# Attention weights of a hybrid decoder turned by transposing DMAs, mask by a maximum in the scan, q, k, v evicted by ScalarE

## The reference, cut to what matters

```python
p = h @ w_in                       # q, k, v (1024 each), pooling input u, gate g
z = q @ k.T / sqrt(128)            # per head, causal key prefix
mask = s_idx < t_idx               # strictly causal
log_1m = where(mask, log_sigmoid(-z), 0.0)
log_stay = reverse_cumsum(log_1m) - log_1m        # sum over s < j < t
wts = where(mask, exp(log_sigmoid(z) + log_stay), 0.0)
a = wts @ v
y = concat([a, pool(u)]) * silu(g);  o = y @ w_out
```

## Time and profile before

| | us |
|---|---|
| three runs | 2297.71, 2519.85, 2673.37 |
| their median | 2519.85 |
| the profiled execution | 2297.7 |
| its span, slowest core | 2296.3 |
| spans of the eight cores | 2288.4 to 2296.3 |

### The profile page before, as it was taken

How to read it: one execution, slowest core, us unless ns; L and a number is a source line. 1 busy time by engine, 2 the same in 40 slices (tenths; PEclk the granted TensorE clock), 3 DMA queues, 4 the chain that set the end, 5 groups by cost and what they waited for, 6 DMA issues and landing times.

```text
span 2296.3 us, 39547 instructions; the slowest of 8 cores (2288.4 to 2296.3 us)
## 1 busy us (share of the span) xinstructions
PE 2198.8 (96%) x13498; PEld 1170.5 (51%) x13740; DVE 1039.8 (45%) x1270; ACT 706.2 (31%) x1378; POOL 624.2 (27%) x616
## 2 busy tenths in 40 slices
PE   5899999999999899999999999999899999999997
PEld 3444566667777444444444555544344444444443
DVE  5500278777777657734443232326632222332222
ACT  3511155555555431134442221243200000002221
POOL 0000055555555421133332333420000000003333
PEclk9999999999999999999999999999999999999999
DMA  9542022222112332944444424436522222583444
GB/s 234 138 65 28 1 30 29 29 30 29 14 18 39 47 56 37 140 136 147 147 148 84 73 44 68 65 45 111 112 37 37 38 37 37 74 131 127 147 158 154
DMA packets 124212, 179.12 MB, mean 78 GB/s; under 512 B 22769, under 2 KB 104945, under 8 KB 113393
## 3 DMA queue, kind: packets, MB, share of 16 engines
q0 software_dynamic: 99344, 71.83, 23.9%
q1 hardware_dynamic: 24674, 104.74, 14.3%
HBM read 198.04 MB, written 33.55 MB: 101 GB/s over the span
## 4 chain that ended last, share of the span: by engine, by line
PE 86%; DMA 5%; issue 2%; DVE 2%; POOL 2%; ACT 1%; SPq 1%; DVEq 0%; POOLq 0%; ACTq 0%
PE ps L267 42%; PE ps L778 17%; PE ps L519 8%; PE ps L537 5%; PE ps L917 3%; PE ps L613 3%; PE ps L601 2%; PE ps L578 2%; DMA yp<-Rc 1%; PE ps L455 1%; SPq L145 1%; POOL xr L800 1%; DMA xr<-x 1%; DMA w1s<-w1s 1%; DMA wg<-w0g 1%
## 5 line engine op out<-in xcount | busy, mean ns | idle before, releaser
L267 PE MATMUL ps<-R,w1s 128*128 128x512 bf16 x2008 | 441.9, 380 | 13.9 <-DMA w1s<-w1s 11.8
L593 POOL TENSOR_TENSOR At<-Cr 128x512 bf16<-128x512 f32 (+1 forms) x320 | 289.9, 912 | 359.2 <-DVE Cr L589 311.2
L267 PEld LDWEIGHTS ps<-R,w1s 128*128 128x128 bf16 x2048 | 200.7, 98 | 255.1 <-issue 14.7
L267 PE MATMUL ps<-R,wg 128*128 128x512 bf16 x1311 | 295.4, 382 | 1.9 <-issue 0.2
L800 POOL TENSOR_TENSOR xr<-xr,tmp 128x512 f32<-128x512 f32 x128 | 162.2, 1267 | 336.3 <-DVE tmp L797 182.3
L519 PE MATMUL ps<-R,wh 128*128 128x512 bf16 x982 | 244.6, 379 | 2.2
L589 DVE TENSOR_TENSOR_SCAN Cr<-ps,Cr,zer 128x512 f32<-128x512 f32 (+1 forms) x192 | 207.8, 1082 | 47.1 <-ACT ps L584 33.1
L584 ACT ACTIVATE ps<-ps 128x512 f32<-128x512 f32 (+1 forms) x320 | 166.0, 519 | 202.4 <-PE ps L578 107.3
L267 PE MATMUL ps<-R,w1c 128*128 128x512 bf16 x1000 | 222.0, 379 | 3.1 <-DVE tmp L797 1.8
L267 PEld LDWEIGHTS ps<-R,wg 128*128 128x128 bf16 x1344 | 131.3, 99 | 156.3 <-issue 6.4
L604 ACT ACTIVATE ATt<-ps 128x512 bf16<-128x512 f32 (+1 forms) x320 | 169.4, 529 | 6.9 <-PE ps L601 6.2
(11 more groups left out here) (130 smaller groups left out, 2339.0 us busy)
## 6 DMA issues: line engine op xcount, KB each, us to landing
xr<-x SPq DMA_DIRECT2D x16, 1024.0 KB, 8.0
x1s<-xr SPq DMA_DIRECT2D x16, 1024.0 KB, 5.4
w1s<-w1s POOLq DMA_DIRECT2D x8, 2048.0 KB, 16.1
xr<-x1s SPq DMA_DIRECT2D x16, 1024.0 KB, 6.9
out<-xr SPq DMA_DIRECT2D x16, 1024.0 KB, 4.8
wh<-w0h POOLq DMA_DIRECT2D x8, 1536.0 KB, 16.0
xt<-x SPq DMA_DIRECT2D x8, 1024.0 KB, 14.0
xq<-x SPq DMA_DIRECT2D x8, 1024.0 KB, 17.8
```

What stands on the lines that cost most here:

```text
L267: fns = [lambda dc=dc: T.matmul(banks[b][:, 0:n], lhsT=w[:, dc, c0:c0 + 128], rhs=rhs[:, dc, lo:lo + n], start=(dc == 0), stop=(dc == 15)) ...
L593: k.op(pool, lambda: G.tensor_tensor(out=a[:, 0:n], in0=C[:, 512 * c:512 * c + n], in1=C[:, 512 * c + 1:512 * c + 1 + n], op=SUB), reads=[ ...
```

## The change

The weights are turned by a DMA with transpose=True, issued by SP one step after `s_z` (LT = 1) into one of five ATt buffers, each with a channel of its own; the identity matmuls L601, their two banks and ACT's copies L604 are gone. `s_v` comes five steps after `s_z` (LV = 5). The banks of `s_z` are now four (0 to 3), and `s_v` accumulates into bank 5 or 4 in turn for successive groups of four rows. The mask matmul is gone; the scan's second operation is a maximum against `msk` (ones on and below the diagonal of the first 128 columns, zeros elsewhere) in a row's first chunk and against one zero column, broadcast, in the others. q, k and v are evicted by ACT. The weight loads within the stage move from step 4 to step 5, the last head's first unit from step 6 to 7. negm and zer are gone; the mask is loaded by POOL's queue ahead of the stage, bones and id32 by SP's after it.

```diff
-    def dma(self, eng, pairs, chan, reads=(), writes=()):
+    def dma(self, eng, pairs, chan, reads=(), writes=(), tp=False):
...
+            if tp:
+                eng.h.dma_start(out=out, in_=in_, transpose=True).then_inc(chan.sem, 16)
...
-            k.dma(sp, [(cst[:], cst_d)], chs, writes=[cstb])
-            for t_, lo in ((identb, 0), (negm, 128), (bones, 256)):
-                k.op(dve, lambda: V.tensor_copy(out=t_[:], in_=cst[:, lo:lo + 128]), reads=[cstb], writes=[cb_])
-            k.op(dve, lambda: V.tensor_copy(out=id32[:], in_=cst[:, 384:416]), reads=[cstb], writes=[cb_])
+            k.dma(sp, [(cst[:], cst_d[:, 0:128])], chs, writes=[cstb])
+            k.op(dve, lambda: V.tensor_copy(out=identb[:], in_=cst[:]), reads=[cstb], writes=[cb_])
...
-        At = [place("At", [128, 512], BF16, 73792 + 1024 * j) for j in range(4)]
-        ATt = [place("ATt", [128, 512], BF16, 69696 + 1024 * j) for j in range(4)]
-        zer, zerb = place("zer", [128, 512], BF16, 77888)
+        At = [place("At", [128, 512], BF16, 74816 + 1024 * j) for j in range(4)]
+        ATt = [place("ATt", [128, 4, 128], BF16, 69696 + 1024 * j) for j in range(5)]
+        tpc = [k.chan() for _ in range(5)]
+        msk, mskb = place("msk", [128, 512], BF16, 78944)
+        mst, mstb = place("mst", [128, 128], F32, 74816)
+        k.dma(pool, [(mst[:], cst_d[:, 128:256])], k.chan(), writes=[mstb])
+        zerw = msk[:, 511:512].broadcast_to([128, 512])
...
+        k.op(dve, lambda: V.memset(msk[:, 128:512], 0.0), writes=[mskb])
+        k.op(dve, lambda: V.tensor_copy(out=msk[:, 0:128], in_=mst[:]), reads=[mstb], writes=[mskb])
...
-                k.op(dve, lambda: V.tensor_copy(out=dst[P][0][:, tg * 512:(tg + 1) * 512], in_=banks[bk]),
+                k.op(act, lambda: A.activation(out=dst[P][0][:, tg * 512:(tg + 1) * 512], in_=banks[bk], func=AF.Copy),
...
-                k.op(dve, lambda: V.tensor_copy(out=Vt[P][0][:, tbg * 4:(tbg + 1) * 4, :],
-                                                in_=banks[bk].rearrange("p (a b) -> p a b", a=4)),
+                k.op(act, lambda: A.activation(out=Vt[P][0][:, tbg * 4:(tbg + 1) * 4, :],
+                                               in_=banks[bk].rearrange("p (a b) -> p a b", a=4), func=AF.Copy),
...
-            P, n, bz = s["h"] % 2, s["n"], s["id"] % 3
+            P, n, bz = s["h"] % 2, s["n"], s["id"] % 4
...
-            if s["first"]:
-                fns.append(lambda: T.matmul(banks[bz][:, 0:128], lhsT=identb[:], rhs=negm[:], start=False, stop=True))
...
+            m1 = msk if c == 0 else zerw
...
-                                                   data1=zer[:, 0:n], initial=ini, op0=MUL, op1=ADD),
+                                                   data1=m1[:, 0:n], initial=ini, op0=MUL, op1=ALU.max),
...
         def s_t(s):
-            n, bt = s["n"], 3 + s["id"] % 2
+            n = s["n"]
             a, ab = At[s["id"] % 4]
-            at, atb = ATt[s["id"] % 4]
-            fns = [lambda q=q: T.matmul(banks[bt][:, q * 128:(q + 1) * 128], lhsT=a[:, q * 128:(q + 1) * 128],
-                                        rhs=identb[:], start=True, stop=True) for q in range(n // 128)]
-            k.op(pe, fns, reads=[ab, cb_], writes=[bankb[bt]])
-            k.op(act, lambda: A.activation(out=at[:, 0:n], in_=banks[bt][:, 0:n], func=AF.Copy),
-                 reads=[bankb[bt]], writes=[atb])
+            at, atb = ATt[s["id"] % 5]
+            k.dma(sp, [(at[:, 0:n // 128, :], a[:, 0:n])], tpc[s["id"] % 5], reads=[ab], writes=[atb], tp=True)
...
+            bv = 5 - (qi // 4) % 2
...
+        LT, LV = 1, 5
+        for t in range(len(steps) + LV):
...
-            if t >= 3 and t - 3 < len(steps):
-                s_t(steps[t - 3])
+            if t >= LT and t - LT < len(steps):
+                s_t(steps[t - LT])
...
-                tgt = max(0, hs - 3) * nun // (per_head - 4)
+                tgt = max(0, hs + 1 - LV) * nun // (per_head - LV)
...
-            if t >= 4:
-                s_v(steps[t - 4])
+            if t >= LV:
+                s_v(steps[t - LV])
+
+        bones, bonesb = place("bones", [128, 128], F32, 79200)
+        id32, id32b = place("id32", [128, 32], F32, 79712)
+        k.dma(sp, [(bones[:], cst_d[:, 256:384])], k.chan(), writes=[bonesb])
+        k.dma(sp, [(id32[:], cst_d[:, 384:416])], k.chan(), writes=[id32b])
```

More of the change, by code:

```diff
@@ L144, in dma @@
             chan.cnt += 16
-            eng.h.dma_start(out=out, in_=in_).then_inc(chan.sem, 16)
+            if tp:
+                eng.h.dma_start(out=out, in_=in_, transpose=True).then_inc(chan.sem, 16)
+            else:
+                eng.h.dma_start(out=out, in_=in_).then_inc(chan.sem, 16)
         tok = Tok(chan.sem, chan.sid, chan.cnt)
@@ L204, in build @@
         AB = R1o + 65536
-        assert AB + 79200 <= 229344, AB
+        assert AB + 80192 <= 229344, AB
         cb_, fmb, epsb = Buf(), Buf(), Buf()
@@ L223, in place @@
             uid["n"] += 1
-            assert off + n <= 79200, (name, off + n)
+            assert off + n <= 80192, (name, off + n)
             return k.place("%s_%d" % (name, uid["n"]), shape, dt, AB + off, n)
@@ L244, in build @@
         chs = k.chan()
-        cst, cstb = place("cst", [128, 416], F32, 77024)
+        cst, cstb = place("cst", [128, 128], F32, 77024)
         k.op(dve, lambda: V.memset(epsc[:], EPS), writes=[epsb])
@@ L597, in s_t @@
         def s_t(s):
[L598 removed]
+            n = s["n"]
             a, ab = At[s["id"] % 4]
[L600 to L605 removed]
+            at, atb = ATt[s["id"] % 5]
+            k.dma(sp, [(at[:, 0:n // 128, :], a[:, 0:n])], tpc[s["id"] % 5], reads=[ab], writes=[atb], tp=True)
         def s_v(s):
             P, n, h, qi = s["h"] % 2, s["n"], s["h"], s["q"]
[L609 removed]
+            at, atb = ATt[s["id"] % 5]
             co = (qi % 4) * 128
+            bv = 5 - (qi // 4) % 2
             nbk = n // 128
             b0 = s["i0"] // 128
[L613 to L614 removed]
+            fns = [lambda j=j: T.matmul(banks[bv][:, co:co + 128], lhsT=Vt[P][0][:, b0 + j, :],
+                                        rhs=at[:, j, :], start=(s["first"] and j == 0),
                                         stop=(s["last"] and j == nbk - 1)) for j in range(nbk)]
             vbs = [vb[P][t] for t in range(b0 // 4, (b0 + nbk - 1) // 4 + 1)]
[L617 removed]
+            k.op(pe, fns, reads=[atb] + vbs, writes=[bankb[bv]])
             if s["last"] and qi % 4 == 3:
@@ L620, in s_v @@
                 yo = y0(h, g * 512, (g + 1) * 512)
-                k.op(dve, lambda: V.tensor_tensor(out=yo, in0=banks[5], in1=yo, op=MUL),
-                     reads=[bankb[5], yb[h][g]], writes=[yb[h][g]])
+                k.op(dve, lambda: V.tensor_tensor(out=yo, in0=banks[bv], in1=yo, op=MUL),
+                     reads=[bankb[bv], yb[h][g]], writes=[yb[h][g]])
         units, nun = [], 0
         g3 = {}
-        for t in range(len(steps) + 4):
+        LT, LV = 1, 5
+        for t in range(len(steps) + LV):
             h, hs = divmod(t, per_head)
@@ L650, in build @@
                 s_z(steps[t])
[L651 to L655, removed]
+            if hs == LV and h < 6:
+                wh_load(h + 2)
+            if hs == LV and h == 6:
                 g3["t"], g3["b"] = place("wg", [128, 16, 512], BF16, 41024)
                 gate_load(3, g3["t"], g3["b"], wgc[0])
-            if hs == 4 and h == 7:
+            if hs == LV and h == 7:
                 wu = {}
@@ L909, in build_w @@
                 in1=wt[:, gg * 36:gg * 36 + 36].unsqueeze(2).broadcast_to([128, 36, 32]), op=MUL),
-                reads=[cb_, wtb], writes=[wb])
+                reads=[id32b, wtb], writes=[wb])
         def conv(gg):
@@ L1195, in prep_weights @@
     cst[:, 0:128] = np.eye(128, dtype=f)
-    cst[:, 128:256] = np.where(p[None, :] <= p[:, None], NEG, 0.0).astype(f)
+    cst[:, 128:256] = np.where(p[None, :] <= p[:, None], 1.0, 0.0).astype(f)
     cst[:, 256:384] = (p[:, None] // 32 == p[None, :] // 32).astype(f) / 1024.0
```

13 lines of the change are left out of this document (4 added, 9 removed).

## The result

The changed kernel takes 2316.9 us (median of 7, 2302.94 to 2633.08), the kernel before, run beside it, 2361.95 (2297.71 to 2715.7). The ratio of the undisturbed runs is 1.0069, 95% interval 1.005 to 1.0089. That is 0.7% slower, which is within 2% and yet clearly not the 2.5% gain that was forecast. The profiled execution of after is 2326.13 us. It is the longest of the six undisturbed executions of after, whose median is 2313.1. Its cores lie further apart: they take 2290.9 to 2324.6 us, those of before 2288.4 to 2296.3. The mean over the cores rises by 15.9 us, from 2291.8 to 2307.7; the other 12.4 of the 28.3 us between the two slowest cores (2324.6 and 2296.3) come from that spread.

The account below looks back on a forecast made before the run. PE's matmul order was taken to bound heads 0 to 6 of the attention stage; 60 + 7 + 10 - 15 - 3 = 59 us less than 2297.7 gave 2240 us (-2.5%), chance 0.47, range 2209 to 2495.

Parts of the forecast that it names:

- beside weight loads: Attention stage's eight stretches with a load: late landings cost 3.8 us each, 30 in all; half, 15, taken, bounds 0 and 30.
- other terms (60 + 7 + 10 - 3): Attention stage: 60 us from transposes off PE, 7 from mask matmuls, 10 from eviction waits, 3 lost at the end.
- The landing: Time for a transposing DMA to land in the attention stage: 3 us alone, 5.3 beside a weight load.
- the cover: Time left between a transposing DMA's issue and s_v's need of its tile, five steps after s_z: some 3.1 us.
- The forecast's own formula: Step beside a weight load: (3.9 chain + 0.2 wake-ups + 5.3 landing)/5 = 1.88 us in place of 1.43.
- The clock: Perhaps a lower granted clock in the attention stage, named as a sign of the second rival; no size given.
- Waits outside loads: PE's wait for the transposed tile: under 20 us in sum and inside weight loads, if the forecast was right.
- The gain of the PE terms: PE's time a head, heads 0 to 6: 66.7 less 7.5 transposes, 1.0 masks, about 1 waits = 57.3 us.
- the wait for L621: PE's wait for the gate eviction, 12.8 us in 24 times, goes with alternating banks; 10 us taken, bounds 6 and 13.
- the first rival: Attention stage: landings of 3.6 to 4.8 us everywhere eat the gain, 2270 to 2310 us; chance 0.17.
- the first price of the second: The second rival at a landing of 5.3 us: 1.82 us a step, 2330 us.
- The second: Rival: transposing DMAs bound the attention stage by landing or issue rate, 2330 to 2495 us; chance 0.33.

Follow-up runs that it names:

- e1: The changed kernel without the weight loads of heads 2 to 7, which reuse the weights of heads 0 and 1: 2264.59 us, ratio to before 0.9841.
- e12: The changed kernel itself measured again, on another chip: ratio to before 1.007.
- e4: The changed kernel with the transposes back on PE with ACT's copies; scan maximum and ACT evictions stay: 2286.87 us, ratio to before 0.9943.
- e5: The changed kernel, loads of heads 2 to 7 and last gate in 16 pieces, pooling's in 20, s_v nine steps behind in heads 0 to 6: 2258.6 to 2271.3 us (cores 0-3).
- e13: The changed kernel, loads of heads 2 to 7 and last gate in 16 pieces, nine steps in heads 0 to 6, pooling loads in a lump: 2264.02 us, ratio 0.9849.
- e14: As e13, but nine steps kept to step 16 of the last head and the last gate's units from its first step: 2253.11 us, ratio 0.9813.

## Why the prediction was wrong

The forecast was 2240, by its sum 59 us under before; measured 0.7% over it. The step that failed is the term "beside weight loads": 15 us for eight loads, bounds 0 and 30. By e1 one load costs 9.3 us (7.7 against the 67.8 of e12), eight some 62 to 74, if the two that stay in e1 cost the same. The forecast's other terms (60 + 7 + 10 - 3) are 74: the term that failed takes back nearly all that PE was to gain. The other terms came out smaller too. With two loads left e1 is 39.9 us under before in the mean of the cores (2291.8 - 2251.9); with some 20 us for those two the change without any load would gain about 60, an estimate, not 74. So the loss is 4 us by the mean of the cores in e12, 16 in the first profile, and the slowest core adds its share.

- *The landing.* Taken as 5.3 us beside a load, from the sixteen Z transfers of the earlier trace rows; measured 7.3 in the median, up to 14. The row's own worst was 8.1, and it was for half the bytes. The profile suggests why, though no run isolates it: the page counts 172449 packets under 512 B where before had 22769. Against e4, which has the transposes on PE, the queue q1 has 149504 packets and 35.7 MB more for the 1088 blocks: an estimated 550 packets of some 240 B for a transposing DMA of four blocks, and each may have to take its turn with the load's larger ones.
- *How it is paid.* I took half of it, as hidden by short steps and the last head. The runs show nothing that hides it: the cover was 3.1 - 2.5 = 0.6 us, At's four buffers stop POOL too, and PE's order lets nothing pass a late s_v. The forecast's own formula with the measured landing, paid in full, gives (3.9 + 0.2 + 7.3)/5 = 2.28 us a step, and over the 17.1 us of a load (7.5 steps x 0.85) 6.4 us, an estimate; the lower clock, which it left out, may make up the rest of the 9.3.
- *The clock.* It was named as a sign of a rival and left out of the sum. Behind a stall it falls (to 0.50 in the stretch from 366 us), and it costs 3.7 us of the 12.6 in the head worked out under e5. In the eight windows that cover 276 to 865 us on core 0 the clock's shortfall adds up to some 85 us at the lower level (twice the shortfall times the length), on core 0 of before some 2.
- *Waits outside loads.* Expected near none; 21 us of PE's 79 in after, and about as much in e1 (35.5 less 13 behind its two loads). The stretch 408 to 414 us of after holds one: the packets of its DMA queues, and its landings, in place of 2.5:

```profile
q1 hardware_dynamic: 1113, 0.26, 41.3%
q14 instruction: 3, 0.02, 3.7%
q8 instruction: 1, 0.02, 1.9%
...
DMA to landing us min/median/max: 3.3/5.1/5.9
```

  Four packets of instruction fetch are all that moves beside the transposes; in 423 to 431 us there are none, and the landings are 2.4 to 2.6. They go together in most such windows, not in all, and no run took the fetches away.
- *What was right.* The gain of the PE terms: 57.3 us a head forecast, 58.0 in two heads of e5 on core 3; the means with their small waits are 60.3 in e5 and 60.1 in e1. No cost of the new scan, none of the evictions, SP's issue (1.2 estimated, 1.19), the wait for L621 gone, DVE at 45 to 46 a head, the rest of the kernel unchanged. By its time (2316.9) the result lies between the first rival (2270 to 2310) and the first price of the second (2330). The first rival's mechanism, a landing of 3.6 to 4.8 us everywhere, is not what happened: the landing is 2.5 us, and 7 in eight short stretches. The second needed 5.3 us or SP's rate everywhere; e1 rules it out. So the sign hung on one term: half of what the nearest row gave, with an upper bound (30) that is itself under half of the 62 to 74 measured.

The forecast cited two pages, one on each side. By the Trainium skill's "Advanced Engine Details and Errata", section "X-Bar Transpose (TRN2)", transposing DMAs are as fast as ordinary ones: alone, the trace doesn't speak against it (2.5 us for 128 KB, 2.0 for a plain DMA of half the size). The 1309 ns a block of the Trainium skill's "VectorE: DVE Perf Modes", section "The three transpose paths", would make four blocks an estimated 5.2 us; the trace's 2.5 decides against multiplying it.

Open: how the eight loads' cost splits between waits and clock on other cores and heads (one head was worked out); whether turn-taking by packets is the mechanism; what e13 and e14 would take without the waits of the last gate's pieces; and a version with no load at all in the stage, which wasn't tried.

## What to carry to other kernels

Work moved from an engine to DMAs that run a fixed distance ahead must be priced by their landing beside the heaviest traffic of the stage, not alone: cover less landing is the slack, and each burst longer than the slack is paid, once a burst, by every engine in the chain, and again in the clock. Cut the other transfers into pieces that nearly fit the slack (16 pieces took 9.3 us to 2.9, 4 pieces gained nothing) and deepen the distance as well; neither gave all of it by itself. Check that the engine that issues the pieces never waits for its own earlier ones, which a dependency helper can add unseen (some 9 us here), and read the spread of the cores, because the slowest of them is the metric.

## What the runs showed of the hardware that was not expected

- A 128x512 bf16 transposing DMA within SBUF lands in 2.2 to 2.5 us alone and costs SP 1.19 us to issue; beside a 1.5 MB casting load (17.1 us) it lands in up to 13.1, beside the pooling stage's loads in up to 14.0, and beside the last gate's load SP's issue stretches to 3.26 us.
- One instruction-fetch stretch with four packets went with landings of 3.3 to 5.9 us.
- One load in 4 bursts costs as much as in one; in 16 it costs a third.
- Behind PE's stalls at the first seven loads, the longest of each 3.0 to 7.1 us, the granted clock fell: the lowest 5 us behind each show 0.50 to 0.64 (core 0 of after). The stalls fall unevenly: in the six undisturbed executions of after the cores lie 14.5 to 33.7 us apart, in the seven of before beside e1 9.8 to 18.0.
